# Two-layer decoder step in split float32: order of the first weights, a gate wait and a square root around the norms

## The reference, cut to what matters

```
x = layer_norm(ALPHA*x + 0.5*swiglu(x, ffn1_in, ffn1_out))      # norm 0
x = layer_norm(ALPHA*x + mixers(x) @ w_out)                      # norm 1
x = layer_norm(ALPHA*x + cross_attention(x, memory) @ w_xo)      # norm 2
x = layer_norm(ALPHA*x + 0.5*swiglu(x, ffn2_in, ffn2_out))      # norm 3
swiglu(h) = (silu(h @ a) * (h @ b)) @ w_out                      # 2816 hidden features
```

## Time and profile before

| | us |
|---|---|
| median of 3 runs (1889.18 to 1896.53) | 1890.41 |
| the profiled execution | 1890.6 |
| its span, first to last instruction | 1888.9 |
| mean granted PE clock, share of full speed | 0.964 |

### The profile page before, as it was taken

How to read it: one execution, slowest core, us unless ns; L and a number is a source line. 1 busy time by engine, 2 the same in 40 slices (tenths; PEclk the granted TensorE clock), 3 DMA queues, 4 the chain that set the end, 5 groups by cost and what they waited for, 6 DMA issues and landing times.

```text
span 1888.9 us, 29843 instructions
## 1 busy us (share of the span) xinstructions
PE 1745.2 (92%) x12302; PEld 1596.8 (85%) x12302; DVE 926.6 (49%) x1497; ACT 667.1 (35%) x929; POOL 114.4 (6%) x220
## 2 busy tenths in 40 slices
PE   7999999977899899999989999998688998999997
PEld 6999998645789589999989999985467886999997
DVE  5554354543564365543455544545446534655534
ACT  3332233332343243432243332433332432433323
POOL 0000100000000000000100001000000000000010
PEclk9999999988899899999989999999988999999998
DMA  7443464586235643433424434636852555344342
GB/s 241 156 145 118 141 225 153 189 323 278 92 123 190 248 153 134 153 131 136 159 94 151 155 115 150 227 134 244 312 222 103 179 202 224 114 151 155 126 140 74
DMA packets 62899, 319.40 MB, mean 169 GB/s; under 512 B 8923, under 2 KB 11355, under 8 KB 37707
## 3 DMA queue, kind: packets, MB, share of 16 engines
q0 software_dynamic: 31104, 205.53, 31.0%
q1 hardware_dynamic: 31690, 112.36, 15.9%
HBM read 307.08 MB, written 10.79 MB: 168 GB/s over the span
## 4 chain that ended last, share of the span: by engine, by line
PE 83%; DVE 7%; DMA 5%; ACT 3%; issue 1%; SPq 1%; DVEq 0%; ACTq 0%
PE ps L578 21%; PE ps L580 21%; PE ps L579 21%; PE ps L545 4%; PE ps L692 2%; PE ps L694 2%; PE ps L693 2%; DMA ring<-in_wkv 2%; PE ps L879 1%; DMA ring<-in_ckv 1%; DVE bn L1406 1%; PE ps L906 1%; PE ps L690 1%; PE ps L689 1%; DMA cache<-in_ckv 1%
## 5 line engine op out<-in xcount | busy, mean ns | idle before, releaser
L578 PE MATMUL ps<-x_high,w_high 128*128 128x320 f32 x1408 | 438.7, 312 | 6.7 <-DVE w_low L1351 6.7
L579 PE MATMUL ps<-x_low,w_high 128*128 128x320 f32 x1408 | 437.4, 311 | 0.0
L580 PE MATMUL ps<-x_high,w_low 128*128 128x320 f32 x1408 | 437.3, 311 | 0.0
L1067 ACT ACTIVATE w_high<-ring 128x2048 fp32r<-128x2048 f32 (+1 forms) x152 | 256.6, 1690 | 472.1 <-PE ps L580 471.4
L1351 DVE TENSOR_TENSOR w_low<-ring,w_high 128x2048 fp32r<-128x2048 f32 (+1 forms) x152 | 305.5, 2011 | 147.2 <-ACT w_high L1067 146.9
L578 PEld LDWEIGHTS ps<-x_high,w_high 128*128 128x128 f32 x1408 | 266.5, 189 | 8.5 <-DVE w_low L1351 7.7
L579 PEld LDWEIGHTS ps<-x_low,w_high 128*128 128x128 f32 x1408 | 266.7, 189 | 0.0
L580 PEld LDWEIGHTS ps<-x_high,w_low 128*128 128x128 f32 x1408 | 266.5, 189 | 0.0
L578 PE MATMUL ps<-h_high,w_high 128*128 128x320 f32 x704 | 220.3, 313 | 6.2 <-DVE h_low L1386 6.2
L514 POOL DMA_DIRECT2D ring<-in_w x216 | 114.2, 529 | 1738.5 <-PE ps L580 1249.3
L580 PE MATMUL ps<-h_high,w_low 128*128 128x320 f32 x704 | 217.5, 309 | 0.0
(11 more groups left out here) (287 smaller groups left out, 2438.0 us busy)
## 6 DMA issues: line engine op xcount, KB each, us to landing
ring<-in_w POOLq DMA_DIRECT2D x152, 1024.0 KB, 5.0
ring<-in_w POOLq DMA_DIRECT2D x64, 704.0 KB, 4.3
cache<-in_dkv SPq DMA_DIRECT2D x64, 256.0 KB, 5.5
ring<-in_dkv SPq DMA_DIRECT2D x64, 256.0 KB, 4.1
cache<-in_ckv SPq DMA_DIRECT2D x8, 2048.0 KB, 10.6
ring<-in_ckv SPq DMA_DIRECT2D x8, 2048.0 KB, 8.3
cache<-in_wkv SPq DMA_DIRECT2D x8, 1536.0 KB, 9.3
ring<-in_wkv SPq DMA_DIRECT2D x8, 1536.0 KB, 9.1
```

The costliest lines, as they stand in the source:

```text
L578: mm(out, wh, xh, start=first, stop=False)
L579: mm(out, wh, xl, start=False, stop=False)
L580: return mm(out, wl, xh, start=False, stop=last)
L1067: fn(w_high[:, pos % 2, 0:n], ring[:, pos % RING, 0:n], ACT.Copy).then_inc(hi_w.sem, 1)
```

## The change

1. `ffn_in` waits at its end for all gated chunks but the last; `project_ffn` waits for the last one in front of block 10 of the second half of its first tile, the block that reads it.
2. At the end of a layer that has a next one, ACT's `norm(3)` makes the high parts of the next layer's slots 0 and 1 in front of the square root, each after waiting for its load and for PE to have used its place; DVE makes the low part of slot 0 in front of the last residual sum, and the x low parts between the odd tiles, as in the other norms. The next layer's start keeps only the low part of slot 1 (all of it stays at the start of layer 0). `high_weights` and `low_weights` get the layer as an argument.
3. In `norm(1)` ACT makes the high part of key half 2 behind the square root and DVE its low part in front of the three normalising instructions, instead of behind them.

The diff, without the places where only the new argument `l` is passed:

```diff
@@ ffn_in (PE)
-                    pe.wait_ge(gate_done.sem, gate_done.upto(l, NF * (u + 1)))
+                    pe.wait_ge(gate_done.sem, gate_done.upto(l, NF * (u + 1) - 1))
@@ project_ffn (PE)
                             for k in range(11):
+                                if m == 0 and half and k == 10:
+                                    pe.wait_ge(gate_done.sem, gate_done.upto(l, NF * (f + 1)))
@@ ACT
-                def high_weights(f, s, add=0):
+                def high_weights(l, f, s, add=0):
...
-                    if s >= 2:
+                    if s >= 2 or (f == 0 and l > 0):
                         act.wait_ge(w_used.sem, w_used.upto(l, pos - 1) + add)
...
-                high_weights(0, 0)
-                high_weights(0, 1)
                 if l == 0:
+                    high_weights(l, 0, 0)
+                    high_weights(l, 0, 1)
@@ norm (ACT)
                     if u == 2:
-                        high_weights(1, 0)
-                        high_weights(1, 1)
+                        high_weights(l, 1, 0)
+                        high_weights(l, 1, 1)
+                    elif u == 3 and l + 1 < L:
+                        high_weights(l + 1, 0, 0)
+                        high_weights(l + 1, 0, 1)
                     act.wait_ge(var_done.sem, var_done.upto(l, u + 1))
                     fn(lnst[:, :, 1], lnst[:, :, 0], ACT.Sqrt, scale=ALPHA ** 2).then_inc(sd_done.sem, 1)
+                    if u == 1:
+                        high_half(H_MK + 2)
                     act.wait_ge(par_done.sem, par_done.upto(l, u + 1))
...
-                norm(1, before=range(H_MK, H_MK + 3))
+                norm(1, before=range(H_MK, H_MK + 2))
@@ norm (DVE)
                         .then_inc(par_done.sem, 1)
+                    if u == 1:
+                        low_half(H_MK + 2)
                     for g, i in ((0, 0), (0, 1), (2, 1)):
...
-                    if u < 3:
+                    if u < 3 or l + 1 < L:
                         low_x(u, pair)
@@ ffn_out (DVE)
                     def ready(m):
                         if m < KD - 1:
-                            low_weights(f, NF + 2 * m + 2)
+                            low_weights(l, f, NF + 2 * m + 2)
+                        elif f == 1 and l + 1 < L:
+                            low_weights(l + 1, 0, 0)
                         dve.wait_ge(w_used.sem, w_used.upto(l, (POS_FFN1, POS_FFN2)[f] + NF + 2 * m + 2))
@@ memory (DVE)
                     for m in range(12):
-                        low_half(H_MK + 2 + m)
+                        if m:
+                            low_half(H_MK + 2 + m)
@@ start of a layer (DVE)
-                for pair in range(4):
-                    low_x(-1, pair)
-                low_weights(0, 0)
                 if l == 0:
+                    for pair in range(4):
+                        low_x(-1, pair)
+                    low_weights(l, 0, 0)
                     bias_rows()
-                low_weights(0, 1)
+                low_weights(l, 0, 1)
```

More of the change, by code:

```diff
@@ L1083, in chunk @@
                         fn(gate[:, j % 2, :], ps[:, 2 * (j % 2), 0:T], ACT.Silu).then_inc(silu_done.sem, 1)
-                        high_weights(u, j + 2, i)
+                        high_weights(l, u, j + 2, i)
                     whole = NF // RING * RING
@@ L1094, in ffn_gate @@
                     for s in range(NF + 2, FFN_SLOTS):
-                        high_weights(u, s)
+                        high_weights(l, u, s)
                 def high_x(u, pair):
@@ L1344, in _, with low_weights @@
                 neglam, sign = cur[:, 128:129], cur[:, 129:130]
-                def low_weights(f, s, add=0):
+                def low_weights(l, f, s, add=0):
                     pos = (POS_FFN1, POS_FFN2)[f] + s
@@ L1387, in chunk @@
                             .then_inc(gate_done.sem, 1)
-                        low_weights(u, j + 2, i)
+                        low_weights(l, u, j + 2, i)
                     whole = NF // RING * RING
@@ L1467, in after @@
                         if m < KD - 1:
-                            low_weights(f, NF + 2 * m + 3)
+                            low_weights(l, f, NF + 2 * m + 3)
                     return ready, after
@@ L1745, in between_xo @@
                     elif m == 6:
-                        low_weights(1, 0)
-                for pair in range(4):
-                    low_x(-1, pair)
-                low_weights(0, 0)
+                        low_weights(l, 1, 0)
                 if l == 0:
+                    for pair in range(4):
+                        low_x(-1, pair)
+                    low_weights(l, 0, 0)
                     bias_rows()
-                low_weights(0, 1)
+                low_weights(l, 0, 1)
                 if l == 0:
@@ L1797, in _ @@
                 norm(2, 1.0, square_out(H_XO), after=between_xo)
-                low_weights(1, 1)
+                low_weights(l, 1, 1)
                 wait_apart(dve, "dve", out_mem.sem, out_mem.upto(l, 32))
```

## The result

The changed kernel took 1866.49 us in the median of four runs (1854.29 to 1871.24); the kernel before took 1889.8 beside it on the same chip. The ratio is 0.9868, 95% interval 0.9827 to 0.991. On the time shown before, that is 1865.5 us (1857.7 to 1873.4), just under the low end of the forecast's range. Run again with more rounds, the same kernel gave 1869.03 us (six runs, 1861.35 to 1874.49) against 1884.43: 0.9912 (0.9886 to 0.9938), or 1873.8 us. So it is faster, by 1.3% in the one measurement and 0.9% in the other (the ratio compares all runs and is not the quotient of the two medians).

The account below looks back on a forecast made before the run. PE was taken to bound the kernel (83% of the chain that ended last). Gains 7.2 + 7.96 + 4.6 + 1.49 = 21.25 us took 1890.60 to 1869.3 us, range about 1865.5 to 1878.

Parts of the forecast that it names:

- Parts 1 and 2: Gated chunk's wait ahead of the down products, gain 4 x 1.8 = 7.2 us; layer boundary, 23.61 to 15.65, gain 7.96 us.
- The four covers: Time to spare: block 21 over 7 us, second down slot's low part 1.5, boundary residual 0.4, square root 0.7.
- So PE doesn't wait: Norm 1: key half 2's low part ready at 536.1, PE needs it at about 536.45; gain 2 x 2.3 us.
- the cover of 0.3 us: Norm 1: time to spare for key half 2's low part before PE needs it, among the three thinnest covers.
- The term of 4.6: Norm 1, one place a layer: PE's idle before key half 2 removed, 2 x 2.3 = 4.6 us, bounds 0 and 5.2.
- Most of the gain comes from DVE's order: Norm 1: the earlier square root alone would move key half 2's low part by only 1.2 us.
- The rival that PE waits in norm 1 for something else: Norm 1: square root isn't what PE waits for, low part still late; 1875.4 us, counted within 0.13 for one part lost.
- Part 3, the clock: First layer's norm 1, key half 2 to 3: 5.56 us becomes 4.07 with the idle gone; gain 1.49, bounds 0 and 1.49.
- for which the two layers' 1.49 is the measure, twice: Range's low end: clock elsewhere allowed 3.0 us beyond part 3's 0.6, 1869.3 - 0.6 - 3.0, about 1865.5.
- The slower rival: Mixers' stretch at a mean clock of 0.74 gives back 30.7 us, ending at 1900 us; chance 0.03.
- The sign named for it: Mixers' stretches: a mean clock under 0.964 would show the prediction wrong.

## Why the prediction was wrong where it was

**Parts 1 and 2: right, term by term.** 7.2 forecast, 7.24 and 7.12 measured; 7.96 forecast, 7.97 and 7.99 measured. The four covers that the forecast named (over 7 us for block 21, 1.5 for the second down slot, 0.4 ahead of the residual sum, 0.7 ahead of the square root) all held, at 1.54, 0.87 and 0.65 for the last three. Taking a distance from norm 2, where the same instructions already stood in the new order, was worth more than adding up the idles: the boundary took 15.64 us in all seven traces that have the new order there. Even such a twin can have a slow form: norm 2 itself took 18.19 once, at a clock of 0.81 (second layer, run with ACT's order alone).

**Part 3, "So PE doesn't wait": wrong.** The step followed one releaser, the low part, through its new place and stopped when it came in time. It did come in time: the cover of 0.3 us that the forecast gave it held, at 0.29. But PE also waits, in front of half 2, for the copy that empties the PSUM bank. The copy was queued on ACT behind 2.57 us of normalising, and in the trace of before it ended at 538.28, 0.40 us ahead of the low part. Worked out from the earlier trace rows with it: high part until 534.89, five normalising instructions 2.57, copy 0.38, some 537.8 instead of 538.68, a gain of about 0.8 where 0.95 came. The term of 4.6 should have been 1.9. "Most of the gain comes from DVE's order" fell with it. The rival that PE waits in norm 1 for something else was on the list, but with the low part as the only thing that could be late; and it was priced all or nothing, at 1875.4, where the case lay between.

**Part 3, the clock: right in its place.** 1.49 forecast, 1.54 measured between half 2 and half 3, with the clock at 1.00 in norm 1 though a wait of 1.45 us remained. The other traces bear it out: with the old norm 1, whose wait is 2.40 us, the slow way (5.55 us) appears in three of six passages, in either layer; with a wait of 1.45 us in none of eight, and without a wait in none of eight. That the kernel before had just one such passage in the profiled execution was a matter of luck, and so was the 1.49. One reading was loose: the matmuls slow down at 539.5, 0.8 us after PE went on, not right behind the idle.

**The range: too narrow below.** With the mis-sized term put right the sum is 18.7, and 1890.6 - 18.7 = 1871.9. The kernel with the copy moved supports this: its two ratios, 0.9885 and 0.9892, stand for about 1869.3, and putting back 2 x 1.4 gives 1872.1. The first four runs of the changed kernel gave 6 us less, the five rounds 2 us more, and both intervals hold 1871.9. So the mis-sized term isn't what took the time below the range; it pulls the other way. The step that failed is "for which the two layers' 1.49 is the measure, twice" (its own sum gives 1865.7, set down as 1865.5). The mixers' stretch, whose instructions are the same in both layers and, norm 1 and the dummies aside, in all these kernels, took from 415.57 to 433.38 us in the traces; already the two layers of the kernel before were 433.38 - 429.22 = 4.16 apart. That was in the trace of before and should have been the measure; counted twice, as the 1.49 was, it puts the low end at 1869.3 - 0.6 - 8.3 = 1860.4. The low end missed by under 0.1 us and the first measurement's own interval reaches over the forecast, so little of the miss says anything of the mechanism, and on which side of the low end the median fell was chance; but the width was argued from one idle, and that was wrong. Whether the change does something more to the stretch than norm 1 shows is not settled: the six passages with the old norm 1 took 423.8 to 433.4 us, the twelve with the new one and no dummies 415.6 to 432.0.

**What the stretch's length goes with.** Mostly the granted clock: at 0.92 and 0.93 it took 432.0 to 433.4 us in three of the stretches shown, at 0.96 it took 415.6 and 425.2; PE's busy time for the same matmuls was 381 to 382 at the one and 369 to 371 at the other. It isn't all of it: 426.54 came at 0.92, and the two at 0.96 differ by 9.6 us of which PE's busy time makes 2.2, the rest being idle. Whether the clock sets the length or goes with something else that does was tried at one place only, with the dummies, and there a higher clock went with 0.7 and 0.9 us less than in the trace beside it; the other places of low clock, around 390 and 460 us, were left alone, and why they are long in one execution and short in the next stays open. The rule of the Trainium skill ("TensorE: Matmul & The Clock Gate", "What's actually happening") that the window is free-running would make such a scatter; no run here tests it.

**The slower rival** had this stretch as its place, and rightly so as to the place: it is what moves from one execution to the next. It didn't decide, since it would have had to take 30.7 us in the two stretches together, and the widest difference of that sum seen is 21.8 (862.60 to 840.78). The sign named for it, a mean clock under 0.964 in the mixers' stretches, came (0.94 and 0.92) and said nothing: 0.964 is the mean of the whole kernel, and the same stretches had 0.93 and 0.94 before the change.

## What to carry to other kernels

When a wait is taken away, list everything that the waiting instruction needs, and for a matmul that includes whoever still reads its PSUM bank and what is queued ahead of that reader; what is latest once the first wait is gone sets the gain. Where the run-to-run scatter sits in one stretch, cut that stretch out of both traces and compare the rest: in the six traces that hold the whole change the rest agrees within 1 us, while the spans differ by 12. And take the width of a range from how far the same instructions already differ within one trace.

## What the runs showed of the hardware that had not been expected

The same 2836 matmuls kept PE busy 368.62 us in one execution and 382.36 in another, and the stretch around them took 415.57 to 433.38 us, without any change to its instructions outside norm 1. Sixteen dummy products in an idle of 4 us brought the granted clock of the ten us behind it from 0.50 to 0.72 and 0.83 in the two layers; thirty of them, over the way to the residual sum, had it at 0.91 and 0.83, took 6.96 us, held PE 2.57 us and made the way no shorter. The clock of 0.50 in norm 1 appeared in three of six passages with an idle of 2.40 us in front and in none of eight with 1.45.
